# Hybrid decoder layer: the first tile's small constants, squares and turned queries put in another order

## The chip, the cores and the metric

One core of a Trainium2 chip runs the whole kernel. The metric is the device time of one execution in microseconds (us), the median of several runs; lower is better.

## What is computed

One layer of a hybrid decoder on 1024 prompt tokens and 32 sample tokens (8 sequences of 4), with a model width of 1024. What matters here is the beginning: normalise the tokens, project them to queries, keys and values, normalise each query and key head, and attend within a window of 128.

```python
def input_branches(x, norm1_g, w_in, q_norm_g, k_norm_g, ln_v_g, ln_v_b):
    h = rms_norm(x, norm1_g)
    z = jnp.einsum("bsd,de->bse", h, w_in)
    ...
    q = rms_norm(q.reshape(b, s, N_KV_HEADS, Q_GROUP, HEAD_DIM), q_norm_g)
    k = rms_norm(k.reshape(b, s, N_KV_HEADS, HEAD_DIM), k_norm_g)
...
def attn_prompt(q, k, v, sinks):
    scores = jnp.einsum("bnqkgd,bnskd->bnkgqs", qb, kk, ...) * (HEAD_DIM ** -0.5)
    p = sink_probs(scores, mask, sinks).astype(vv.dtype)
    o = jnp.einsum("bnkgqs,bnskd->bnqkgd", p, vv).reshape(b, s, ATTN_WIDTH)
```

After it come a gated spatial mixing, the merge of both branches, and a mixture of 16 experts with two per token. All of that is left as it is.

## The kernel before

The tokens are worked in nine tiles: eight of 128 prompt tokens (tile 0 to 7, `PT` is 8) and one of the 32 sample tokens. Five engines run their own instruction lists side by side and meet on semaphores; each list is written out by hand in the order in which it is issued, and an engine that waits holds up all that stands behind it in its list. SP issues the DMAs (lines 286 to 370), POOL takes the powers of -0.5 for the norms and subtracts half of the roundings, ACT copies and squares, PE multiplies and turns (transposes), DVE scales, subtracts and reduces.

Each float32 product is made of three products of reduced-precision parts (`product`, lines 65 to 74, whose three matmuls are lines 71 to 73): high by high, high by low, low by high. So each weight tile that lands is rounded by ACT into `w_hi` (line 569), and DVE makes `w_lo`, what the rounding left (lines 1034 and 1044). The weights for queries, keys and values are six tiles of 512 KB, loaded in the order `W_ORDER`: the two of keys and values, then the four of queries. Line 306 issues them. Ahead of the last two (`n == NP - 2`) SP also issues the rows of tile 1 (`load_x(1)`, line 293, which waits until ACT has normalised tile 0).

Behind the weights SP issues the transposed tokens of tile 1 (`load_xT(1)`, line 300), and then 14 small DMAs (lines 308 to 318), all on the semaphore `const_in`: the gains of the query and key norms, turned into a column one number per partition (`qk_gain`, four DMAs), the key gain and the attention sinks spread over all partitions, and the sinks of the sample tile (`s_sinks`, eight DMAs). Then come the rows and the transposed tokens of tiles 2 to 8, each behind a wait of its own: the rows of tile t reuse one buffer and wait for the squares of tile t-1 (`x_squared`).

The first tile, as the lists have it:

- PE: `first_kv` (24 matmuls), `first_q(0)` (24; the first two query weight tiles), `spread_rstd(1)`, `first_q(1)` (24; the last two), `qk_turn(0)` (four transposes of queries, one of keys; lines 722 and 723), `spread_rstd(2)`, `scores(0, 0)` (line 737). Then for each tile s from 1: `project_kv(s)`, `scores(s - 1, 1)`, `project_q(s, ...)` with the turns of the probabilities and the values of tile s-1 between its parts, `qk_turn(s)`, `dens_turn(s - 1)`, `spread_rstd(s + 2)`, `scores(s, 0)`.
- ACT: the squares of tile 0, its normalisation, the six `w_hi` with the high part of tile 0's h and the squares of tile 1 between them, `diagonal(1)` (line 493), `copy_kv(0)` (lines 517 to 522), the squares of tile 2 (`square(2)`, line 480), `h_high(1)` (line 498), `copy_q(0)` (line 506, then the squares of the queries, line 510), `diagonal(2)`, `copy_qT(0)` (line 535: the turned queries from PSUM to `qT`, times the gain), `square(3)`.
- DVE: the low parts of the weights, the last two in line 1044, then it waits for all 14 constants (line 1047), scales the query gain (line 1048), `k_squares(0)` (lines 943 and 944), `k_scale(0)`, `h_scale(1)` (line 934, eight instructions, which need tile 1's transposed tokens and its spread norm), `mean_square(2)` (line 917), `q_squares(0)`, `copy_kT(0)` (line 975). Then `mask_scores(0, 0)`, `h_scale(2)`, `mask_scores(0, 1)` and so on.
- POOL: for each s the root of the keys' squares, `rstd(s + 2)` (line 389), `h_low(s + 1)` (line 396), the root of the queries' squares (line 401).

The norm of a later tile goes a long way: ACT squares its rows, DVE takes the mean, POOL the root, ACT scales a unit matrix by it (`diagonal`), PE multiplies it by ones to spread it over the partitions (`spread_rstd`, line 660), and DVE reads that in `h_scale`.

`scores(t, gp)` works on two of the four query groups: gp 0 on groups 0 and 1, gp 1 on groups 2 and 3. It waits for `qT_copied` and for `kT_copied`. Both scores of a tile read the one `qT` that one ACT instruction fills.

Of the kernel before, what the change touches and what calls it, by code (L numbers as in the profile page):

```python
# [129 lines left out]
def attention_phase(nc, io, keep, psum):  # L130
# [7 lines left out]
    with ExitStack() as ctx:  # L138
# [148 lines left out]
        def _(sp):  # L287
# [13 lines left out]

            load_x(0)
            for n, c in enumerate(W_ORDER):
                if n == NP - 2:
                    load_x(1)
                sp.dma_start(raw[c], w_tile(io, c)).then_inc(w_in[c], DMA)
            load_xT(1)
            for half in range(2):
                part = slice(HD * half, HD * half + HD)
                sp.dma_start(qk_gain[part, 0:1], io["q_norm_g"].rearrange("a d -> d a")).then_inc(const_in, DMA)  # L310
                sp.dma_start(qk_gain[part, 1:2], io["k_norm_g"].rearrange("a d -> d a")).then_inc(const_in, DMA)
            sp.dma_start(k_gain[:, :], io["k_norm_g"][0].partition_broadcast(P)).then_inc(const_in, DMA)
            sp.dma_start(sinks[:, :], io["attn_sinks"][0].partition_broadcast(P)).then_inc(const_in, DMA)
            for g in range(G):
                for kv in range(KV):
                    h = kv * G + g
                    sp.dma_start(s_sinks[32 * g:32 * g + 32, kv:kv + 1],
                                  io["attn_sinks"][0, h:h + 1].partition_broadcast(32)).then_inc(const_in, DMA)
# [54 lines left out]
        def _(pool):  # L373
# [52 lines left out]
            for s in range(NT):  # L426
# [3 lines left out]
                if s + 2 < NT:  # L430
                    rstd(s + 2)
                if s + 1 < NT:
                    h_low(s + 1)
                if s < PT:
                    q_root(s)
                if 1 <= s <= G:
# [36 lines left out]
        def _(act):  # L473
# [50 lines left out]
            def copy_qT(t):  # L524
# [5 lines left out]

                if t < PT:
                    out = qT[:, :, 0:n]
                else:
                    out = qT[:, 0, :].rearrange("p (g n) -> p g n", g=G)
                act.activation(out, bank(psum, 4).rearrange("p (g n) -> p g n", g=G)[:, :, 0:n], ACT.Copy,
                               scale=qk_gain[:, 0:1]).then_inc(qT_copied, 1)
# [45 lines left out]
            square(2)  # L582
            for s in range(NT):
# [12 lines left out]
                else:  # L596
# [5 lines left out]
                    if s == 0:  # L602
                        copy_q(s)
                    if s + 2 < NT:
# [3 lines left out]
                    copy_qT(s)  # L608
# [32 lines left out]
        def _(pe):  # L641
# [71 lines left out]
            def qk_turn(t):  # L713
# [5 lines left out]
                if t >= 1:  # L719
                    pe.wait_ge(qT_copied, t)  # L720
# [5 lines left out]
            def scores(t, gp):  # L726
# [3 lines left out]
                pe.wait_ge(qT_copied, t + 1)  # L730
# [48 lines left out]
            def sample_scores():  # L779

                pe.wait_ge(sq_spread, 1)
                pe.wait_ge(qT_copied, NT)
# [1716 lines left out]
```

## Time and profile before

| what | us |
|---|---|
| median of three runs | 957.81 |
| lowest and highest of them | 956.85, 958.0 |
| the profiled execution's own time | 960.3 |
| its span in the trace | 958.2 |
| PE busy | 914.7 (95%) |
| DVE, ACT, POOL busy | 460.0, 356.4, 218.1 |

The span runs from the first to the last instruction of the profiled execution; 2.1 us of its own time lie around it. A busy PE is one with a matmul under way, be it at the full or the half clock. In a timeline a row is an instruction or several equal ones merged, with its start, its duration, and in brackets how long the engine was idle before it and what ended that. The mean granted clock of TensorE over the span is 0.979 of full speed.

### The profile page before, as it was taken

The page shows a single profiled execution, that of the slowest core. Times are in us where ns is not written, and L with a number is a line of the kernel's source. Part 1 is how long each engine was busy: PE and PEld are TensorE (multiplying, and loading weights), DVE is VectorE, ACT ScalarE, POOL GpSimd, SP SyncE. Part 2 cuts the span into 40 slices and gives each one's busy share as a digit, 9 for nine tenths or more (in the row PEclk, how much of TensorE's full clock was granted, in tenths as well). Part 3 has the DMA queues.
Part 4 walks back from the last instruction along what each step waited for, and adds up shares of the span by engine and source line. Part 5 has one row for each costly group of instructions (what it writes and reads, how often), then busy time and mean ns, then how long its engine had stood idle before and what let it go on. Part 6 is the DMA issues. An engine that isn't in the chain of part 4 may idle for free. (4 is left out here: it accounts for less than half of the span.)

```text
span 958.2 us, 16289 instructions
## 1 busy us (share of the span) xinstructions
PE 914.7 (95%) x5425; PEld 825.2 (86%) x5426; DVE 460.0 (48%) x842; ACT 356.4 (37%) x614; POOL 218.1 (23%) x241
## 2 busy tenths in 40 slices
PE   7899998999998999999999999999999999999993
PEld 7677776787998999999999999999887888888882
DVE  4587876433222222231232254443895768577550
ACT  5566555210232111111111141221425667577551
POOL 1434222345120000000000020000032347354552
PEclk9899999999999999999999999999899999999997
DMA  7321310200302102101110025863357898989833
GB/s 243 92 85 45 112 59 19 73 1 1 102 1 69 65 33 66 33 33 66 33 66 33 22 87 190 305 240 95 95 196 250 282 329 281 310 264 318 261 52 45
DMA packets 59247, 118.57 MB, mean 124 GB/s; under 512 B 9357, under 2 KB 34637, under 8 KB 59184
## 3 DMA queue, kind: packets, MB, share of 16 engines
q1 hardware_dynamic: 50672, 100.10, 30.4%
q0 software_dynamic: 7488, 17.85, 8.2%
q8 instruction: 28, 0.46, 0.2%
q10 hardware_dynamic: 1040, 0.00, 0.1%
q14 instruction: 19, 0.16, 0.1%
HBM read 105.37 MB, written 23.00 MB: 134 GB/s over the span
## 5 line engine op out<-in xcount | busy, mean ns | idle before, releaser
L1411 ACT ACTIVATE gate<-psum 128x352 f32<-128x352 f32 x48 | 22.2, 465 | 209.9 <-PE psum L73 209.9
L71 PE MATMUL psum<-w_hi,hT_hi 128*128 128x512 f32 (+3 forms) x224 | 84.4, 377 | 3.9 <-DVE hT_lo L1037 2.0
L73 PE MATMUL psum<-w_hi,hT_lo 128*128 128x512 f32 (+3 forms) x224 | 80.5, 359 | 0.0
L72 PE MATMUL psum<-w_lo,hT_hi 128*128 128x512 f32 (+3 forms) x224 | 80.3, 358 | 0.0
L2173 DVE TENSOR_TENSOR hT_lo<-room,hT_hi (+1 forms) x32 | 72.0, 2289 | 16.4 <-ACT hT_hi L1875 16.4
L71 PE MATMUL psum<-hT_hi,x_xT_hi 128*128 x192 | 77.5, 404 | 1.8 <-DVE x_xT_lo L2349 1.5
L71 PE MATMUL psum<-hT_hi,w_hi 128*128 128x352 f32 x240 | 77.4, 323 | 0.0
L72 PE MATMUL psum<-hT_lo,w_hi 128*128 128x352 f32 x240 | 76.9, 321 | 0.0
L73 PE MATMUL psum<-hT_hi,w_lo 128*128 128x352 f32 x240 | 76.9, 320 | 0.0
L72 PE MATMUL psum<-hT_lo,x_xT_hi 128*128 x192 | 75.2, 392 | 0.0
L73 PE MATMUL psum<-hT_hi,x_xT_lo 128*128 x192 | 75.1, 391 | 0.0
L1812 POOL DMA_INDIRECT out_y<-y,put_at x23 | 44.3, 1925 | 97.2 <-DMA out_y<-y,put_at 79.5
L1875 ACT ACTIVATE hT_hi<-room (+1 forms) x32 | 59.9, 1921 | 14.2 <-PE psum L73 12.6
L71 PE MATMUL psum<-hT_hi,g_w_hi 128*128 128x352 f32 x192 | 62.7, 326 | 2.1 <-PEq L1326 2.1
L1769 POOL MEMSET c_zeros<- 128x128 f32 x1 | 0.2, 204 | 277.7 <-POOLq L1326 277.7
L73 PE MATMUL psum<-hT_hi,g_w_lo 128*128 128x352 f32 x192 | 62.2, 324 | 0.0
L72 PE MATMUL psum<-hT_lo,g_w_hi 128*128 128x352 f32 x192 | 62.2, 324 | 0.0
L1491 DVE TENSOR_TENSOR room<-psum,gate 128x352 f32 (+1 forms) x24 | 12.5, 524 | 97.6 <-ACT gate L1411 97.6
L71 PEld LDWEIGHTS psum<-w_hi,hT_hi 128*128 128x128 f32 (+1 forms) x224 | 42.2, 188 | 15.0 <-issue 9.0
L71 PE MATMUL psum<-hT_hi,o_w_hi 128*128 128x352 f32 x168 | 54.8, 326 | 0.0
L73 PE MATMUL psum<-hT_hi,o_w_lo 128*128 128x352 f32 x168 | 54.2, 323 | 0.0
L72 PE MATMUL psum<-hT_lo,o_w_hi 128*128 128x352 f32 x168 | 54.2, 323 | 0.0
(347 smaller groups left out, 2329.6 us busy)
## 6 DMA issues: line engine op xcount, KB each, us to landing
room<-in_w_gu SPq DMA_DIRECT2D x16, 2048.0 KB
dn_raw<-in_w_dn SPq DMA_DIRECT2D x16, 1024.0 KB
g_w_raw<-in_w_ab SPq DMA_DIRECT2D x15, 768.0 KB, 4.3
xT_chunk<-in_xT SPq DMA_DIRECT2D x8, 528.0 KB, 3.7
x_in<-in_x SPq DMA_DIRECT2D x8, 512.0 KB, 4.1
out_y<-y SPq DMA_DIRECT2D x8, 512.0 KB, 3.3
hn_rows<-squares SPq DMA_DIRECT2D x8, 512.0 KB, 3.2
o_w_raw<-in_w_out_t SPq DMA_DIRECT2D x7, 512.0 KB, 6.6
```

The source lines that it names most:

```text
L71: eng.matmul(out, lh, rh, start=first and k == 0, stop=False)
L72: eng.matmul(out, lh, rl, start=False, stop=False)
L73: mm = eng.matmul(out, ll, rh, start=False, stop=last and k == nk - 1)
L1411: act.activation(gate[:, (ab + c) % 2, :], bank(psum, gate_pair(ab, c))[:, 0:TC], ACT.Sigmoid).then_inc(gated.sem, 1)
L1491: dve.tensor_tensor(out, bank(psum, gate_pair(ab, c) + 1)[:, 0:TC].unsqueeze(1), gate[:, (ab + c) % 2, :].unsqueeze(1), ALU.mult).then_inc ...
L1769: pool.memset(c["zeros"][:, :], 0.0).then_inc(zeros_made, 1)
L1812: pool.indirect_dma_start(io["y"], bass.IndirectOffsetOnAxis(put_at[:, j:j + 1], 0), out[:, j, :], None, bounds_check=NTOK - 1, oob_is_err ...
L1875: act.activation(gu_hi[:, buf, ks], gu_raw[:, buf, ks], ACT.Copy).then_inc(gu_hi_made.sem, 1)
L2173: dve.tensor_tensor(gu_lo[:, buf, ks], gu_raw[:, buf, ks], gu_hi[:, buf, ks].bitcast(F32), ALU.subtract).then_inc(gu_lo_made.sem, 1)
```

## The change

- SP: the 14 small DMAs move from behind `load_xT(1)` to between `load_x(1)` and the last two query weight tiles.
- ACT: `square(2)` moves from ahead of `h_high(1)` to behind `copy_q(0)` and `copy_qT(0)`; in the first tile `copy_qT(0)` also comes ahead of `diagonal(2)`.
- ACT: `copy_qT` of a prompt tile is two instructions, two groups each; `scores(t, gp)` waits for its own half (`u + 1` is 2t + gp + 1). The other waits on `qT_copied` are renumbered.
- DVE: `mean_square(2)` moves from ahead of `q_squares(0)` to behind `copy_kT(0)`. POOL: `rstd(2)` moves behind `h_low(1)` and the root of tile 0's queries. PE: `spread_rstd(2)` moves from ahead of `scores(0, 0)` to behind `project_kv(1)`.
- The condition `0 < s < NT - 2` on POOL's first `rstd` leaves all tiles but s = 0 as they were.

```diff
--- before.py
+++ after.py
@@ -299,23 +299,26 @@
                     sp.wait_ge(h_scaled, 2 * (t - 1))
                 sp.dma_start(xT_tile[t % 2][:, :, 0:rows(t)], io["xT"][:, :, toks(t)]).then_inc(xT_came[t % 2], DMA)
 
+            def load_constants():
+                for half in range(2):
+                    part = slice(HD * half, HD * half + HD)
+                    sp.dma_start(qk_gain[part, 0:1], io["q_norm_g"].rearrange("a d -> d a")).then_inc(const_in, DMA)
+                    sp.dma_start(qk_gain[part, 1:2], io["k_norm_g"].rearrange("a d -> d a")).then_inc(const_in, DMA)
+                sp.dma_start(k_gain[:, :], io["k_norm_g"][0].partition_broadcast(P)).then_inc(const_in, DMA)
+                sp.dma_start(sinks[:, :], io["attn_sinks"][0].partition_broadcast(P)).then_inc(const_in, DMA)
+                for g in range(G):
+                    for kv in range(KV):
+                        h = kv * G + g
+                        sp.dma_start(s_sinks[32 * g:32 * g + 32, kv:kv + 1],
+                                      io["attn_sinks"][0, h:h + 1].partition_broadcast(32)).then_inc(const_in, DMA)
+
             load_x(0)
             for n, c in enumerate(W_ORDER):
                 if n == NP - 2:
                     load_x(1)
+                    load_constants()
                 sp.dma_start(raw[c], w_tile(io, c)).then_inc(w_in[c], DMA)
             load_xT(1)
-            for half in range(2):
-                part = slice(HD * half, HD * half + HD)
-                sp.dma_start(qk_gain[part, 0:1], io["q_norm_g"].rearrange("a d -> d a")).then_inc(const_in, DMA)
-                sp.dma_start(qk_gain[part, 1:2], io["k_norm_g"].rearrange("a d -> d a")).then_inc(const_in, DMA)
-            sp.dma_start(k_gain[:, :], io["k_norm_g"][0].partition_broadcast(P)).then_inc(const_in, DMA)
-            sp.dma_start(sinks[:, :], io["attn_sinks"][0].partition_broadcast(P)).then_inc(const_in, DMA)
-            for g in range(G):
-                for kv in range(KV):
-                    h = kv * G + g
-                    sp.dma_start(s_sinks[32 * g:32 * g + 32, kv:kv + 1],
-                                  io["attn_sinks"][0, h:h + 1].partition_broadcast(32)).then_inc(const_in, DMA)
             for t in range(2, NT):
                 load_x(t)
                 load_xT(t)
@@ -427,12 +430,14 @@
                 if s == PT:
                     q_root(s)
                 k_root(s)
-                if s + 2 < NT:
+                if 0 < s < NT - 2:
                     rstd(s + 2)
                 if s + 1 < NT:
                     h_low(s + 1)
                 if s < PT:
                     q_root(s)
+                if s == 0:
+                    rstd(s + 2)
                 if 1 <= s <= G:
 
                     pool.wait_ge(z_rstd, 2 * s + 2)
@@ -528,12 +533,14 @@
                 if t >= 1:
                     act.wait_ge(s_made, 2 * t)
 
+                src = bank(psum, 4).rearrange("p (g n) -> p g n", g=G)
                 if t < PT:
-                    out = qT[:, :, 0:n]
+                    for gp in range(2):
+                        gs = slice(2 * gp, 2 * gp + 2)
+                        act.activation(qT[:, gs, :], src[:, gs, :], ACT.Copy, scale=qk_gain[:, 0:1]).then_inc(qT_copied, 1)
                 else:
-                    out = qT[:, 0, :].rearrange("p (g n) -> p g n", g=G)
-                act.activation(out, bank(psum, 4).rearrange("p (g n) -> p g n", g=G)[:, :, 0:n], ACT.Copy,
-                               scale=qk_gain[:, 0:1]).then_inc(qT_copied, 1)
+                    act.activation(qT[:, 0, :].rearrange("p (g n) -> p g n", g=G), src[:, :, 0:n], ACT.Copy,
+                                   scale=qk_gain[:, 0:1]).then_inc(qT_copied, 1)
 
             def probs(t, gp):
                 u = 2 * t + gp
@@ -579,7 +586,6 @@
                 act.activation(w_hi[:, :, c * P:(c + 1) * P], vs_raw[c], ACT.Copy).then_inc(vs_hi_made, 1)
 
             copy_kv(0)
-            square(2)
             for s in range(NT):
                 done = s - 1
                 if s == PT:
@@ -601,11 +607,13 @@
                     h_high(s + 1)
                     if s == 0:
                         copy_q(s)
+                        copy_qT(s)
+                        square(s + 2)
                     if s + 2 < NT:
                         diagonal(s + 2)
                     if s > 0:
                         copy_q(s)
-                    copy_qT(s)
+                        copy_qT(s)
                     if s > 0:
                         copy_rT(done)
                     if s + 3 < NT:
@@ -717,7 +725,7 @@
                 if t == PT:
                     pe.wait_ge(sq_normed, 1)
                 if t >= 1:
-                    pe.wait_ge(qT_copied, t)
+                    pe.wait_ge(qT_copied, 2 * t)
                 for g in range(G):
                     pe.transpose(bank(psum, 4)[:, g * P:g * P + n], z[0:n, g * P:(g + 1) * P], ident[0:n, 0:n])
                 pe.transpose(bank(psum, 1)[:, KT_AT:KT_AT + n], k_norm[0:n, :, :].rearrange("p k d -> p (k d)"),
@@ -727,7 +735,7 @@
 
                 u = 2 * t + gp
                 k0 = block_keys(t)
-                pe.wait_ge(qT_copied, t + 1)
+                pe.wait_ge(qT_copied, u + 1)
                 pe.wait_ge(kT_copied, t + 1)
                 if u >= 1:
                     pe.wait_ge(s_ready, u)
@@ -779,7 +787,7 @@
             def sample_scores():
 
                 pe.wait_ge(sq_spread, 1)
-                pe.wait_ge(qT_copied, NT)
+                pe.wait_ge(qT_copied, 2 * PT + 1)
                 pe.wait_ge(kT_copied, NT)
                 pe.wait_ge(k_cache_in, DMA)
                 pe.wait_ge(s_ready, 2 * PT)
@@ -855,10 +863,11 @@
             spread_rstd(1)
             first_q(1)
             qk_turn(0)
-            spread_rstd(2)
             scores(0, 0)
             for s in range(1, PT):
                 project_kv(s)
+                if s == 1:
+                    spread_rstd(s + 1)
                 scores(s - 1, 1)
                 project_q(s, 0, 4)
                 probs_turn(s - 1, 0)
@@ -1055,7 +1064,7 @@
             def spread_q():
 
                 dve.wait_ge(spread_zeroed, 1)
-                dve.wait_ge(qT_copied, NT)
+                dve.wait_ge(qT_copied, 2 * PT + 1)
                 dve.tensor_scalar(spread(qT_spread), bank(psum, 4).rearrange("p (g n) -> p g n", g=G)[:, :, 0:NS]
                                   .rearrange("p g (b t) -> p b g t", b=DEC_B), qk_gain[:, 0:1], None,
                                   ALU.mult).then_inc(sq_spread, 1)
@@ -1063,9 +1072,9 @@
             k_squares(0)
             k_scale(0)
             h_scale(1)
-            mean_square(2)
             q_squares(0)
             copy_kT(0)
+            mean_square(2)
             for s in range(1, NT):
                 done = s - 1
                 mask_scores(done, 0)
```

## Rows read from the trace of the kernel before

**Rows 1.** The page: busy time of each engine, and the chain that ended last.

```profile
PE 914.7 (95%) x5425; PEld 825.2 (86%) x5426; DVE 460.0 (48%) x842; ACT 356.4 (37%) x614; POOL 218.1 (23%) x241
...
PE 36%; DVE 2%; DMA 1%; issue 1%; POOL 0%; ACT 0%; DVEq 0%; POOLq 0%; ACTq 0%
```

**Rows 2.** Timeline of PE: start us, us, instruction [idle before <-releaser].

```profile
19.63 0.36 PE L71 MATMUL psum<-w_hi,hT_hi 128*128 128x256 f32 x1
...
22.48 0.27 PE L73 MATMUL psum<-w_hi,hT_lo 128*128 128x256 f32 x1
26.30 0.79 PE L722 MATMUL psum<-ident,z_qkv 128*128 128x128 f32 x4 [3.54 <-ACT z_qkv L506]
...
28.68 1.23 PE L737 MATMUL psum<-kT,qT 64*128 64x128 f32 x8 [0.63 <-DVE kT L975]
...
34.50 0.72 PE L737 MATMUL psum<-kT,qT 64*128 64x128 f32 x8
...
45.18 1.14 PE L737 MATMUL psum<-kT,qT 64*128 64x256 f32 x8 [0.46 <-ACT qT L535]
```

**Rows 3.** Timeline of ACT in the first tile.

```profile
16.31 1.06 ACT L569 ACTIVATE w_hi<-sp_sb 128x1024 fp32r<-128x1024 f32 x1 [0.33 <-DMA sp_sb<-in_w_tiles]
...
23.20 1.06 ACT L480 ACTIVATE x_in<-x_in 128x1024 f32<-128x1024 f32 x1 [4.51 <-DMA x_in<-in_x]
...
25.13 0.63 ACT L498 ACTIVATE hT_hi<-h_raw 128x512 fp32r<-128x512 f32 x1 [0.26 <-DVE h_raw L934]
25.67 0.58 ACT L506 ACTIVATE z_qkv<-psum 128x512 f32<-128x512 f32 x1
...
27.34 0.69 ACT L535 ACTIVATE qT<-psum,qk_gain 128x512 f32<-128x512 f32 x1
...
34.61 0.28 ACT L517 ACTIVATE z_qkv<-psum 128x128 f32<-128x128 f32 x1 [5.53 <-PE psum L73]
```

**Rows 4.** Timeline of DVE in the first tile.

```profile
16.11 2.52 DVE L1044 TENSOR_TENSOR w_lo<-sp_sb,w_hi 128x1024 fp32r<-128x1024 f32 x2
21.38 0.15 DVE L1048 TENSOR_SCALAR qk_gain<-qk_gain 128x1 f32<-128x1 f32 x1 [2.75 <-DMA s_sinks<-in_attn_sinks]
...
22.95 2.15 DVE L934 SCALAR_TENSOR_TENSOR h_raw<-x_in,g,psum 128x128 f32<-128x128 f32 x8
...
28.19 0.34 DVE L975 TENSOR_SCALAR kT<-psum,qk_gain 128x128 f32<-128x128 f32 x1
```

**Rows 5.** Timeline of SP's queue: one row is the issue of one or several DMAs.

```profile
7.73 0.33 SPq L293 DMA_DIRECT2D x_in<-in_x  x1
8.10 0.91 SPq L306 DMA_DIRECT2D sp_sb<-in_w_tiles  x2
...
9.76 2.27 SPq L310 DMA_DIRECT2D qk_gain<-in_q_norm_g  x1
...
15.13 3.68 SPq L317 DMA_DIRECT2D s_sinks<-in_attn_sinks  x8
18.86 0.42 SPq L293 DMA_DIRECT2D x_in<-in_x  x1
```

**Rows 6.** DMA issues: rows of tile 3 at 24.38, xT of tile 2 at 19.32; us to landing.

```profile
x_in<-in_x SPq DMA_DIRECT2D x1, 512.0 KB, 3.5
...
x_norm<-in_xT SPq DMA_DIRECT2D x1, 512.0 KB, 5.5
```

**Rows 7.** Stretches of PE: length, busy (instructions), granted clock, DMA share, GB/s.

```profile
13.00:16.40 3.40, 3.40 (x19) 0.50 0.90 270
26.60:33.40 6.80, 6.17 (x31) 0.51 0.57 189
```

**Rows 8.** Timelines of ACT, DVE and PE around the turn of tile 2.

```profile
60.88 0.69 ACT L535 ACTIVATE qT<-psum,qk_gain 128x512 f32<-128x512 f32 x1 [0.45 <-PE psum L723]
...
61.27 0.34 DVE L975 TENSOR_SCALAR kT<-psum,qk_gain 128x128 f32<-128x128 f32 x1
...
61.71 1.14 PE L737 MATMUL psum<-kT,qT 64*128 64x256 f32 x8 [0.20 <-ACT qT L535]
```

## The prediction

> **What bounds the kernel now.** I began with the page's busy times and its chain [rows 1]: PE is busy for 95% of the span, and of the chain only PE has a share that counts. So any microsecond by which PE's list is moved in the first tile is passed on to the end, as long as no wait further on takes it up. Next I read PE's timeline of the first tile [rows 2]. PE has its third product (`first_q(1)`) done at 22.75 us, then stands idle until 26.30, where the turn starts on ACT's copy of the queries. From there to `scores(0, 0)` at 28.68 it is idle again for 0.63 us, on DVE's copy of the turned keys.
>
> Why is that copy late? ACT's timeline [rows 3] has it at 25.67, right behind the second half of h of tile 1. Ahead of that ACT waited 4.51 us for tile 2's rows (23.20), whose squares stand in its list. But h of tile 1 came only when DVE had scaled it: DVE's timeline [rows 4] has the last low part of the weights done at 18.63, then 2.75 us of waiting for the constants, the gain at 21.38 and the eight scalings from 22.95 to 25.10. Both waits have one root: SP's queue [rows 5]. The constants are issued from 9.76 to 18.81, 9.05 us for 14 DMAs, the first alone 2.27. Tile 2's rows, free to go since tile 1's squares, go behind them at 18.86. So SP's time of issue is what the first tile pays for. The constants land late for DVE, the rows late for ACT, and DVE's chain is the one that ends last.
>
> **The moved constants.** The 14 issues now stand ahead of the last two weight tiles, which SP issued at 8.10 (both in 0.91 us). For the 14, my bounds are 9.05 us as measured and 7.24 us, which has the first at the 0.46 us of a sink's issue (3.68 / 8 in [rows 5]; 9.05 - 2.27 + 0.46). I take the short one: the 2.27 came when six loads had been issued ahead of it and few were through, now there are fewer. The last weight tile is then issued at 8.10 + 7.24 + 0.45 = 15.8 us, at the latest at 17.6, where it was 8.55. It lands 3.5 us later if it goes as fast as a load alone, 5.5 if like the second of a pair [rows 6]. It is the second of a pair, with tile 1's transposed tokens behind it, so I take 5.5. Call the landing L: 21.3 us, between 19.3 and 23.1. Before, ACT had it at 16.31.
>
> The Trainium skill, "DMA: Bandwidth & Descriptors", section "Issuing engines are not separate DMA queues", says that the time to initiate a DMA on its sequencer is usually small beside the DMA itself. By that the move would delay the weights hardly at all. The rows above say otherwise here for small transfers, but it is the second rival below.
>
> What hangs on L: DVE has the last low part 2.32 us after ACT starts on the tile (16.31 to 18.63), so `first_q(1)`, which began at 19.63 without a wait for weights, now begins at L + 2.4 = 23.7, after 4 us of idle PE. It took 3.0 us at the full clock. The granted clock was 0.50 from 13.0 to 16.4 after an idle stretch of 2 us, and again from 26.6 to 33.4 after the 3.54 us [rows 7]. So this product will run mostly at the half clock, 1.2 GHz. `project_kv(1)`, as many matmuls, took 4.6 us mostly at that level (29.91 to 34.50 in [rows 2]). I take 4.6, which gives queries at L + 7.0. Ends: 3.0 and, all doubled, 6.0.
>
> The other chain: the constants are in by then, so DVE takes up the gain at L + 2.3. From the gain to the end of `h_scale(1)` is 25.10 - 21.38 = 3.7 us [rows 4], then 0.57 for ACT's last half of h [rows 3]: ACT could copy the queries at L + 6.6. `copy_kv(0)` now also stands behind the late weight tile on ACT, and is done before DVE is free, so it adds nothing. Tile 1's transposed tokens are issued at 16.3 and needed at L + 3.9 = 25.2, which is 9 us. The later of both chains is PE's: the copy starts at L + 7.1 = 28.4 against 25.67, **+2.7 us**. With the bounds of L and 6.6 to 8.5 behind it, the copy lies between +0.2 and +5.9.
>
> **The squares, the diagonal and the rest of tile 2's norm.** The squares leave ACT's way ahead of h: that was a wait of 4.51 us, but its cover was DVE's late h, so it is worth 0 (the second half waited for DVE by 0.26 as it was). With the copy of the keys unchanged in its place, from ACT's copy of the queries to `scores(0, 0)` stays 28.68 - 25.67 = 3.0 us. `diagonal(2)` ahead of `copy_qT(0)` cost nothing, since that copy began at 27.34 as the turn ended. `spread_rstd(2)` leaves PE ahead of the scores, where PE waited for keys anyway: 0. What is late next: `square(3)` waits in ACT's list for rows that are issued only after `square(2)`, now about when the scores begin, and land 3.5 us later [rows 6]. `copy_kv(1)` stands behind it. In the trace it came 5.9 us after the scores (34.61 in [rows 3]), which leaves room for the 3.5 and the 1.06 of the squares. Only when PE is fast does this bite, by 0 to 0.4 us. `h_scale(2)` on DVE now waits for a matmul behind `project_kv(1)`; what DVE does next, `mask_scores(0, 1)`, needs scores that PE makes behind that same product and so waited there before too: 0.
>
> **The halved copy of the queries.** It can bring only what `scores` waits for `qT` beyond `kT`. At tile 2 `qT` is done at 61.57 and `kT` at 61.61 [rows 8], PE goes at 61.71: the wait of 0.20 that the trace puts down to ACT ends with DVE. The tiles repeat this, with waits of 0.2 (0.46 at tile 1, [rows 2]), and by their order `kT` hangs on the squares of the queries, which the change doesn't touch. So **0**; if the attribution were right, at most the 0.3 us by which half a copy of 0.69 is shorter, at seven tiles: 2.1 us at the very most, 1.6 by the waits that there are (0.46 and six times 0.2). The second instruction lengthens ACT's list by 0.1 to 0.2 us a tile, which ACT's idle time covers (37% busy in [rows 1]).
>
> **What the clock gives back.** After `scores(0, 0)` PE ran on at the half clock until 33.4: those scores took 1.23 where the second ones took 0.72, `project_kv(1)` 4.6 where `first_q(1)` took 3.0. Together that is 2.1 us. If PE's new burst from 23.7 to 28.3 brings the full clock back in time, all of it comes back, less the 0.4 of `square(3)`; if the idle stretches around the turn take it away once more, nothing does. I take 1.2, between the ends 0 and 2.1.
>
> **Sum.** +2.7 - 1.2 + 0 = +1.5 us on 960.3 for the profiled execution, which stood 2.5 above the median. On the median it is 957.81 + 1.5 = **959.3**. A measurement of this kernel tells 0.2% from nothing, 1.9 us, so the forecast case is "the same, rather slower".
>
> **Rivals.**
> 1. *The queue stalls as before* (slower). The first constant takes its 2.27 us again, behind x of tile 1 and two weight tiles in flight, L is 23.1, and PE's longer idle leaves the half clock on through `project_kv(1)`. Then +2.7 + 1.8 - 0 to 1.2: +3.3 to +4.5, or 961.1 to 962.3. For it: the 9.05 us is what was measured. It decides from 0.4 us above my sum. Chance 0.27.
> 2. *The weights don't wait* (faster). If issuing were cheap here, as by the skill's rule, the last tile would land as at 16.3, `first_q(1)` would end at 22.75, and the early constants would give DVE's chain 2.75 us. ACT copies at 22.9, -2.8, and with no idle PE the clock stays, up to -2.1 more: 952.9 to 955.0. Against it: SP issued tile 2's rows only behind the last constant, though nothing else held them. Chance 0.10.
> 3. *Early landing and a quick clock*: L at 19.3 to 20 and all 2.1 us back, -1.9 to +0.1, or 955.9 to 957.9. Chance 0.15.
> The forecast case, 0 to +3.2, has 0.48.
>
> **The numbers.** Slower by over 0.2%: 0.27 and the upper quarter of the forecast case, 0.12, is 0.39. Faster by over 0.2%: 0.10 and 0.04 of the third rival, 0.14. Between: 0.47. The range leaves out the second rival and the last part of the first: 956.4 to 962.3. The forecast case alone is 957.8 to 961.0.
>
> **What would show it.** In the changed trace: SP issues the last two weight tiles at 15 to 17.6 us; ACT's `w_hi` of the last starts at L; PE idle of about 4 us ahead of the second half of the queries' product, with a granted clock near 0.50 after it; DVE's wait for constants gone, its wait for the last weights in its place; `copy_q(0)` at 28.4, the scores at 31.4. The step is wrong if SP's issues take well under 7 us, or if the last tile lands before 19. The clock term is right if the start of `scores(1, 0)`, 45.18 before [rows 2], moves by about 1.5. From there on all tiles should keep their 16.5 us (61.71 - 45.18), with waits before `scores` of the same 0.2; if those waits vanish, the halved copy did count.

## The result, and the profile after

The changed kernel takes 961.2 us in the median of 20 runs (958.32 to 963.19), the kernel before 958.8 in 20 runs beside them (956.85 to 961.33). The ratio is 1.0021, 95% interval 1.0012 to 1.003: 2.0 us slower, with 1.2 to 2.9 as its bounds (the two medians lie 2.4 us apart). A second comparison gave 1.0012 (0.9995 to 1.0029), which by itself is not clear of nothing.

The profiled execution doesn't show this by itself. It took 960.29 us (span 958.1), as long as the one of before (960.3, span 958.2); before's was 1.5 us above its own median, after's 0.9 below. So first what its parts show, then which of them lasts. The page:

```profile
PE 912.1 (95%) x5425; PEld 822.3 (86%) x5426; DVE 460.9 (48%) x842; ACT 357.2 (37%) x622; POOL 225.2 (24%) x241
...
PE 36%; DVE 2%; DMA 1%; issue 1%; POOL 0%; ACT 0%; DVEq 0%; POOLq 0%; ACTq 0%
```

PE is the bound as in [rows 1]. SP's queue, which answers to [rows 5]:

```profile
7.77 0.33 SPq L293 DMA_DIRECT2D x_in<-in_x  x1
...
8.14 0.58 SPq L305 DMA_DIRECT2D qk_gain<-in_q_norm_g  x1
...
11.77 3.70 SPq L312 DMA_DIRECT2D s_sinks<-in_attn_sinks  x8
...
15.51 0.90 SPq L320 DMA_DIRECT2D sp_sb<-in_w_tiles  x2
...
17.10 0.66 SPq L293 DMA_DIRECT2D x_in<-in_x  x1
```

The 14 constants take from 8.14 to 15.47, 7.3 us, the first of them 0.58 and not 2.27. The last two weight tiles go at 15.51 where they went at 8.10. ACT and DVE, which answer to [rows 3, 4]:

```profile
19.19 1.06 ACT L576 ACTIVATE w_hi<-sp_sb 128x1024 fp32r<-128x1024 f32 x1 [5.30 <-DMA sp_sb<-in_w_tiles]
...
20.54 1.06 ACT L576 ACTIVATE w_hi<-sp_sb 128x1024 fp32r<-128x1024 f32 x1 [0.30 <-DMA sp_sb<-in_w_tiles]
...
27.27 0.60 ACT L511 ACTIVATE z_qkv<-psum 128x512 f32<-128x512 f32 x1
...
28.73 0.84 ACT L540 ACTIVATE qT<-psum,qk_gain 128x256 f32<-128x256 f32 x2 [0.20 <-PE psum L731]
...
33.98 1.06 ACT L485 ACTIVATE x_in<-x_in 128x1024 f32<-128x1024 f32 x1 [1.83 <-DMA x_in<-in_x]
```

```profile
20.27 2.58 DVE L1053 TENSOR_TENSOR w_lo<-sp_sb,w_hi 128x1024 fp32r<-128x1024 f32 x2 [4.04 <-ACT w_hi L576]
...
22.77 0.15 DVE L1057 TENSOR_SCALAR qk_gain<-qk_gain 128x1 f32<-128x1 f32 x1
...
24.33 2.15 DVE L943 SCALAR_TENSOR_TENSOR h_raw<-x_in,g,psum 128x128 f32<-128x128 f32 x8
...
29.37 0.34 DVE L984 TENSOR_SCALAR kT<-psum,qk_gain 128x128 f32<-128x128 f32 x1
```

ACT's wait has changed its name. It was 4.51 us for tile 2's rows at 23.20; it is 5.30 us for a weight tile at 19.19. DVE's wait of 2.75 us for the constants is gone, and a wait of 4.04 for the weights stands ahead of 20.27. The gain comes at 22.77, 1.4 us later than before. PE, which answers to [rows 2], and its granted clock, which answers to [rows 7]:

```profile
21.94 0.62 PE L668 MATMUL psum<-qT_spread 128*128 128x128 f32 x2 [2.55 <-ACT qT_spread L498]
...
23.00 0.55 PE L71 MATMUL psum<-w_hi,hT_hi 128*128 128x256 f32 x1 [0.44 <-DVE w_lo L1053]
...
27.93 0.66 PE L730 MATMUL psum<-ident,z_qkv 128*128 128x128 f32 x4 [0.69 <-ACT z_qkv L511]
...
29.86 0.72 PE L745 MATMUL psum<-kT,qT 64*128 64x128 f32 x8 [1.17 <-DVE kT L984]
...
33.77 0.71 PE L745 MATMUL psum<-kT,qT 64*128 64x128 f32 x8
...
44.53 1.14 PE L745 MATMUL psum<-kT,qT 64*128 64x256 f32 x8 [0.46 <-ACT qT L540]
```

```profile
22.20:25.60 3.40, 2.96 (x14) 0.50 0.84 260
26.60:33.40 6.80, 4.95 (x43) 1.00 0.24 77
```

PE's idle stretch now lies ahead of the second half of the queries' product, and the half clock (1.2 GHz) falls on that product, from 22.2 to 25.6. `project_kv(1)`, which ran at the half clock before [rows 7], runs at the full one (2.4 GHz). So `scores(0, 0)` starts 1.18 us later than before, and `scores(1, 0)` 0.65 earlier (44.53 against 45.18).

### The profile page after: what moved, and what is told of

The parts are those of the page before. It is cut to its first block and busy times, and to the rows that moved or that the text cites. A ratio compares the mean times of both kernels' runs of the same rounds, so it can differ in the third digit from the quotient of the medians.

```text
span 958.1 us, 16297 instructions
## 1 busy us (share of the span) xinstructions
PE 912.1 (95%) x5425; PEld 822.3 (86%) x5426; DVE 460.9 (48%) x842; ACT 357.2 (37%) x622; POOL 225.2 (24%) x241
## 5 line engine op out<-in xcount | busy, mean ns | idle before, releaser
L1420 ACT ACTIVATE gate<-psum 128x352 f32<-128x352 f32 x48 | 22.2, 464 | 210.1 <-PE psum L73 210.0
L1821 POOL DMA_INDIRECT out_y<-y,put_at x23 | 46.5, 2023 | 89.7 <-DMA out_y<-y,put_at 71.0
```

Source lines behind the costliest of these rows:

```text
L1420: act.activation(gate[:, (ab + c) % 2, :], bank(psum, gate_pair(ab, c))[:, 0:TC], ACT.Sigmoid).then_inc(gated.sem, 1)
L1821: pool.indirect_dma_start(io["y"], bass.IndirectOffsetOnAxis(put_at[:, j:j + 1], 0), out[:, j, :], None, bounds_check=NTOK - 1, oob_is_err ...
```

## The experiments

All traces in one table, in us. "S0" is the start of `scores(0, 0)`, "S1" that of `scores(1, 0)`; between them lie 16.50 us in [rows 2]. The ratios are to the kernel before, run on the same chip.

| kernel | gain on DVE | S0 | S1 | S1 - S0 | median (runs) | ratio (95%) |
|---|---|---|---|---|---|---|
| before, first trace | 21.38 | 28.68 | 45.18 | 16.50 | 958.8 (20) | |
| before again | 20.41 | 28.70 | 45.72 | 17.02 | 960.38 (12) | 1.0013 (0.999 to 1.0036) |
| after, first trace | 22.77 | 29.86 | 44.53 | 14.67 | 961.2 (20) | 1.0021 (1.0012 to 1.003) |
| after again | 22.73 | 30.02 | 45.77 | 15.75 | 959.96 (11) | 1.0012 (0.9995 to 1.0029) |
| constants alone | 22.72 | 30.03 | 44.40 | 14.37 | 961.12 (7) | 1.0035 (1.002 to 1.005) |
| all but the constants | 19.98 | 26.83 | 42.96 | 16.13 | 958.86 (12) | 1.0007 (0.9996 to 1.0019) |
| half copies alone | 19.59 | 27.09 | 43.70 | 16.61 | 959.56 (12) | 1.0014 (1.0003 to 1.0024) |
| after, six constants ahead | 19.60 | 26.45 | 43.66 | 17.21 | 958.39 (12) | 0.9993 (0.9977 to 1.0009) |
| before, PE kept busy | 20.26 | 27.57 | 41.93 | 14.36 | 954.49 (6) | 0.9958 (0.9942 to 0.9973) |
| after, PE kept busy | 22.61 | 29.79 | 44.37 | 14.58 | 958.45 (11) | 0.9995 (0.9987 to 1.0004) |
| constants on ACT | 20.33 | 29.07 | 45.97 | 16.90 | 961.65 (11) | 1.002 (1.0005 to 1.0035) |
| the same, PE kept busy | 20.51 | 29.26 | 43.63 | 14.37 | 960.52 (12) | 1.0012 (1.0001 to 1.0022) |
| sinks late | 19.24 | 27.89 | 43.71 | 15.82 | 958.34 (11) | 0.9991 (0.9978 to 1.0004) |
| the same, PE kept busy | 18.40 | 27.07 | 41.44 | 14.37 | 955.61 (8) | 0.9961 (0.9947 to 0.9975) |

The kernel before against itself reads 1.0013, with an interval that holds 1. Differences of 0.1% between two lines are therefore not to be read. The traces' times of S0 and S1 are finer, but each is one execution, and S0 of one and the same kernel differs by the landing of its loads.

### The change taken apart

Constants alone: the 14 DMAs are moved as in the change, nothing else is.

```diff
                 if n == NP - 2:
                     load_x(1)
+                    load_constants()
...
-            for half in range(2):
...
```

> Only the 14 constants are moved ahead of the last two weight tiles. Theory A (the weights are late because SP's issues take 7.4 us): all of the change's loss is here, +1.2 to +3 us against before (ratio 1.001 to 1.003), the last weight tile starts on ACT at 20 to 21 us, scores(0, 0) at about 29.9 where it was 28.68. Rival B (the loss comes from tile 2's later norm or from the two half copies): no slower than before, ratio 0.998 to 1.0005.

All of the loss is here: 1.0035, a little above the forecast range, with S0 at 30.03 and the last weight tile on ACT at 20.49. That is theory A's case, and B falls. S1, at 44.40, is as early as in the changed kernel and earlier than before's 45.18, so the loss that the medians show is not to be seen at S1 of this trace.

All but the constants: `load_constants()` is called behind `load_xT(1)`, as the 14 were before (the edit is against the changed kernel).

```diff
                     load_x(1)
-                    load_constants()
...
             load_xT(1)
+            load_constants()
```

> All of the change except for the constants, which stay behind the transposed tokens of tile 1. Theory A: within 0.5 us of before, since DVE still waits for the constants until 21.4 us and ACT's copy of the queries hangs on that (25.6 to 25.7 us). Rival B: +1 to +2.5 us, with copies or norms late at each tile. A third reading (ACT's wait of 4.5 us for tile 2's rows was what held the copy): -1 us or more, the copy well before 25 us.

No loss (1.0007). But S0 is at 26.83, 1.85 us earlier than in before, and the copy of the queries at 24.27, where theory A had 25.6. The first trace of before was a late one, it turned out: here the last constant was there at 19.98, not 21.38, and from the gain to the copy it is 4.29 us in both. So this trace doesn't tell whether ACT's wait for the rows (the third reading) counts. The kernel before, unchanged, for a second trace:

> The kernel before, unchanged, against itself, for a second profile: ratio 1 within 0.001. The first trace has the last constant at 21.4 us; the parts' traces, with the same SP order, have it at 19.6 to 20.3. If that first trace was a late one: the gain at 19.5 to 20.5 here, scores(0, 0) at 26.8 to 27.6. If the first was typical: 21.4 and 28.7.

The gain came early, at 20.41, and S0 did not follow: 28.70, as in the first trace. The rows of this trace (timelines of DVE, ACT and PE):

```profile
20.41 0.15 DVE L1048 TENSOR_SCALAR qk_gain<-qk_gain 128x1 f32<-128x1 f32 x1 [1.92 <-DMA s_sinks<-in_attn_sinks]
...
23.84 1.06 ACT L480 ACTIVATE x_in<-x_in 128x1024 f32<-128x1024 f32 x1 [3.98 <-DMA x_in<-in_x]
...
25.94 0.57 ACT L506 ACTIVATE z_qkv<-psum 128x512 f32<-128x512 f32 x1
...
26.56 0.66 PE L722 MATMUL psum<-ident,z_qkv 128*128 128x128 f32 x4 [3.83 <-ACT z_qkv L506]
...
28.70 1.22 PE L737 MATMUL psum<-kT,qT 64*128 64x128 f32 x8 [0.69 <-DVE kT L975]
```

DVE is through with h of tile 1 at 24.13, but ACT waited 3.98 us for tile 2's rows and squared them until 24.9. Then came two halves of h and only then the queries, at 25.94. With the squares out of the way ACT could have copied them 0.57 us behind DVE's h, at 24.7: the squares held the copy by 1.2 us. So in the kernel before two waits are nearly level, the constants' and the squares', and which ends last differs from one execution to the next. Where the squares are moved (all but the constants) S0 was at 26.83; where they are not and the rows came early (half copies alone, ACT's squares at 21.94) at 27.09, as DVE's chain allows.

Half copies alone: only `copy_qT` and its waits.

```diff
+                    for gp in range(2):
+                        gs = slice(2 * gp, 2 * gp + 2)
+                        act.activation(qT[:, gs, :], src[:, gs, :], ACT.Copy, scale=qk_gain[:, 0:1]).then_inc(qT_copied, 1)
...
-                pe.wait_ge(qT_copied, t + 1)
+                pe.wait_ge(qT_copied, u + 1)
```

> Only the turned queries of a prompt tile are copied in two halves. By the prediction 0 (within 0.3 us): scores hang on the turned keys, and the waits before scores stay 0.2 and 0.46 us. If the trace's attribution of these waits to the queries were right: up to -1.6 us, and the waits gone. If ACT's longer list counts: up to +1 us.

```profile
42.61 0.84 ACT L535 ACTIVATE qT<-psum,qk_gain 128x256 f32<-128x256 f32 x2 [0.19 <-PE psum L725]
...
43.26 0.34 DVE L977 TENSOR_SCALAR kT<-psum,qk_gain 128x128 f32<-128x128 f32 x1
...
43.70 1.13 PE L739 MATMUL psum<-kT,qT 64*128 64x256 f32 x8 [0.47 <-ACT qT L535]
```

Two instructions take 0.84 us where one took 0.69, and the wait of 0.47 before the scores of tile 1 is what it was (0.46 in [rows 2]): it ends with DVE's turned keys (43.26 + 0.34). From the scores of tile 1 to those of tile 7 it is 99.20 us in the traces of before and after and 99.22 here, so a tile neither gains nor loses. The ratio, 1.0014, leans to the slow side; nothing in this trace answers to that, and the kernel before reads the same against itself.

The changed kernel, unchanged, for a second trace:

> The changed kernel, unchanged, for a second profile on a chip with the kernel before: scores(0, 0) at 29.7 to 30.1 again, since its end hangs on SP's issues and not on the last constant; ratio 1.001 to 1.003. Rival: it spreads as the first trace of before did, and the ratio is 1 within 0.001.

S0 is at 30.02, beside 29.86: the changed kernel's first tile hardly spreads, as its end hangs on SP's issues. What spreads is the stretch behind it, 15.75 us in place of 14.67:

```profile
31.91 0.41 ACT L498 ACTIVATE qT_spread<-ident,xrs 128x128 f32<-128x128 f32 x1 [1.15 <-POOL xrs L392]
...
35.20 1.06 ACT L485 ACTIVATE x_in<-x_in 128x1024 f32<-128x1024 f32 x1 [2.89 <-DMA x_in<-in_x]
...
36.26 0.26 ACT L522 ACTIVATE z_qkv<-psum 128x128 f32<-128x128 f32 x1
...
38.57 0.66 PE L756 MATMUL psum<-ident,sp_sb 128*128 128x128 f32 x4 [0.93 <-ACT sink_e L554]
```

ACT waits 2.89 us for tile 3's rows, which are issued only when tile 2's are squared. The copy of tile 1's keys stands behind them at 36.26, the probabilities behind that, and PE waits 0.93 us ahead of their turn. In the first trace of after the same wait was 1.83 us and PE had none there. This is the moved squares' own price; with the constants alone, where the squares were not moved, S1 - S0 is 14.37.

### How much of the weights' delay is SP's time of issue

The changed kernel with only six constants ahead of the weights; the eight sinks, which the sample tile alone needs, follow `load_xT(2)` on a semaphore of their own.

```diff
-        N_CONST = 6 + G * KV
+        N_CONST = 6
...
+            def load_sinks():
                 for g in range(G):
...
                 load_xT(t)
+                if t == 2:
+                    load_sinks()
...
+            dve.wait_ge(sinks_in, DMA * G * KV)
             step.did(dve.tensor_tensor(top[:, 0:KV], s_top[:, :], s_sinks[:, :], ALU.max))
```

> The changed kernel, but only the 6 constants that the first tile needs are ahead of the last two weight tiles; the 8 sinks of the sample tile go behind the transposed tokens of tile 2, on a semaphore of their own. Theory A: the issues ahead of the weights fall from 7.4 to 3.5 us, the last weight tile is there at 16.5 to 17.5 us (the DMA engines are then the limit), DVE starts on the gain at about 19.5, scores(0, 0) at 26 to 27 us: 2 to 4 us faster than before (ratio 0.996 to 0.998). Rival B: no faster than before.

```profile
11.75 0.91 SPq L323 DMA_DIRECT2D sp_sb<-in_w_tiles  x2
...
17.36 1.06 ACT L581 ACTIVATE w_hi<-sp_sb 128x1024 fp32r<-128x1024 f32 x1 [0.29 <-DMA sp_sb<-in_w_tiles]
...
19.60 0.15 DVE L1062 TENSOR_SCALAR qk_gain<-qk_gain 128x1 f32<-128x1 f32 x1
...
24.51 0.66 PE L735 MATMUL psum<-ident,z_qkv 128*128 128x128 f32 x4 [1.59 <-ACT z_qkv L516]
...
26.45 1.23 PE L750 MATMUL psum<-kT,qT 64*128 64x128 f32 x8 [1.17 <-DVE kT L989]
```

```profile
25.60:32.40 6.80, 5.96 (x30) 0.50 0.49 152
```

SP's part came out as theory A had it: 3.8 us less of issue, the last tile 3.2 us earlier (17.36 against 20.54), S0 3.4 us earlier. The time did not come out as expected: 0.7 us faster than before and not clear of it, where 2 to 4 were expected. Against the changed kernel's 1.0021 it is 2.7 us better, so the eight sinks ahead of the weights carry the loss. PE's idle stretches (1.59 ahead of the turn, 1.17 ahead of the scores) now lie behind the queries' product again, and the half clock falls on the scores and on `project_kv(1)`, 25.6 to 32.4. S1 is at 43.66, so S1 - S0 took 17.21 us, 2.85 more than in the traces at the full clock below (14.36). Of the 3.4 us that the weights' earlier landing gained at S0 over the changed kernel, 0.9 are left at S1 (43.66 against 44.53).

### The clock held still

To see the late weights without the half clock behind them, PE is kept busy in its idle stretches by matmuls of the unit matrix by itself into an unused bank (`warm_up`, which the kernel has for its start). Nothing reads their result. In the kernel before:

```diff
             first_q(1)
+            warm_up(14)
             qk_turn(0)
             spread_rstd(2)
+            warm_up(4)
             scores(0, 0)
```

> The kernel before, with 14 matmuls of the unit matrix by itself in PE's idle stretch ahead of the turn of tile 0 and 4 ahead of its first scores (their result is not used). They are to keep the full clock. Theory A: from scores(0, 0) to scores(1, 0) takes 14.4 us in place of 16.5, as in the changed kernel, and the kernel is 1 to 2 us faster than before (ratio 0.998 to 0.999). If the half clock costs nothing at the end: within 0.5 us of before.

```profile
25.65 0.60 PE L722 MATMUL psum<-ident,z_qkv 128*128 128x128 f32 x4
...
27.57 0.72 PE L737 MATMUL psum<-kT,qT 64*128 64x128 f32 x8
...
31.25 0.72 PE L737 MATMUL psum<-kT,qT 64*128 64x128 f32 x8
...
41.93 1.13 PE L737 MATMUL psum<-kT,qT 64*128 64x256 f32 x8 [0.47 <-ACT qT L535]
```

```profile
26.60:33.40 6.80, 6.75 (x56) 1.00 0.47 145
```

The clock stays at 1.00 where it was 0.51 in [rows 7], S1 - S0 is 14.36 in place of 16.50, and the kernel takes 954.49 us: ratio 0.9958, 4 us faster, twice the most that was expected. S0, at 27.57, is early for another reason than the clock: the constants and tile 2's rows were there early (the gain at 20.26, the squares at 22.01), and from the copy of the queries to S0 it is 3.0 us as in the first trace of before. This trace also lacks a stretch of half clock near 170 us that the first traces of before and after both have (0.50 from 170.0 and from 168.9, for 3.4 us each); behind it 1.6 us more are gained. Whether that comes of the new order in time or of chance, one trace doesn't tell. The profiled execution (953.06 us) was also the fastest of its six.

In the changed kernel, where the idle stretches are others:

```diff
+            warm_up(18)
             spread_rstd(1)
             first_q(1)
+            warm_up(4)
             qk_turn(0)
+            warm_up(7)
             scores(0, 0)
```

> The changed kernel, with 18 such matmuls ahead of spread_rstd(1), 4 ahead of the turn and 7 ahead of scores(0, 0). With the clock kept up in both, what is left between this and the kernel before with its own such matmuls is the late weights alone. Theory A: 2.5 to 3 us slower than that one, with scores(0, 0) at 29.5 to 30 us, and about level with before (ratio 0.9995 to 1.0015). Rival (the change's loss was the clock's): level with the kernel before that has them.

```profile
27.53 0.66 PE L730 MATMUL psum<-ident,z_qkv 128*128 128x128 f32 x4
...
29.79 0.71 PE L745 MATMUL psum<-kT,qT 64*128 64x128 f32 x8
...
44.37 1.13 PE L745 MATMUL psum<-kT,qT 64*128 64x256 f32 x8 [0.46 <-ACT qT L540]
```

S0 is where it was (29.79), S1 too. Side by side on one chip, both at the full clock between S0 and S1, the two orders differ by 2.2 us at S0, 2.4 at S1 and 4.0 in the medians (954.49, 958.45), where 2.5 to 3 were expected. What the medians have beyond the 2.4 lies behind S1: the trace of the changed kernel has the stretch of half clock near 170 us, and the other hasn't. The rival, that the change's loss was the clock's, falls: with PE kept busy in both the changed order is still the slower one, and by more.

### Other places for the constants

Six constants issued by ACT at its very start, where it waits for tile 0's rows, and the sinks late as above, without and with PE kept busy (4 ahead of the turn, 4 ahead of the scores).

```diff
             act.dma_start(g1[:, :], io["norm1_g"][0].rearrange("(k p) -> p k", p=P)).then_inc(g1_in, DMA)
+            for half in range(2):
+                part = slice(HD * half, HD * half + HD)
+                act.dma_start(qk_gain[part, 0:1], io["q_norm_g"].rearrange("a d -> d a")).then_inc(const_in, DMA)
...
```

> The kernel before, with the 6 constants of the first tile issued by ACT at its start, where it waits for tile 0's rows, and the 8 sinks of the sample tile behind the transposed tokens of tile 2 on SP. Nothing stands ahead of the weights, and DVE waits for no constant. Theory A: the last weight tile on ACT at 15 to 16.5 us, the gain at 18.7, the copy of the queries at 22.9, scores(0, 0) at 25.5: 1.5 to 3 us faster than before (ratio 0.997 to 0.9985). It fails if ACT's six issues (3.5 us) hold up the squares of tile 0, which begin at 4.5: then later by that much.

> The same as the one with ACT's constants, with 4 matmuls of the unit matrix ahead of the turn and 4 ahead of scores(0, 0). Theory A: clock kept up, scores(1, 0) at about 40 us where the kernel before has 43 to 45: 3 to 5 us faster than before (ratio 0.995 to 0.997). If the clock stays up without them: the same as without.

```profile
5.17 1.28 ACT L485 ACT_TABLE_LOAD   x1 [5.02 <-issue]
...
6.47 1.06 ACT L485 ACTIVATE x_norm<-x_in 128x1024 f32<-128x1024 f32 x1
```

ACT's issues last until 5.14, and the load of its table, which used to run while the rows were on their way, comes only then: the squares of tile 0 start at 6.47 and not at 4.52. Tile 0 starts 1.95 us late. The expectation had named this as what could spoil it. Without the added matmuls the kernel is slower than before (1.002). With them it is not faster (1.0012, no more than before reads against itself), and the first tile does not explain that: S1 is at 43.63, 1.55 us earlier than in the first trace of before, and that lead is still 1.58 us among the last experts (an ACT copy at 887.39 that stood at 888.97). It goes just behind:

```profile
895.05 1.03 ACT L1935 ACTIVATE y<-psum 128x1024 f32<-128x1024 f32 x1 [3.56 <-POOLq L1819]
```

In the first trace of before this row stands at 893.68, behind a wait of 0.61. ACT copies an expert's output here, and may do so only when POOL has seen its last scatter-add into `y` land. Behind it, at PE's last wait for an expert (943.08 against 941.14), the lead of 1.6 us has become a lag of 1.9. A lead of the first tile can so be spent at the end, on a DMA; that this wait alone did it was not tried.

Six constants left on SP behind the weights, as before, and only the sinks late, without and with PE kept busy:

> The same order of the constants without the added matmuls. Theory A: scores(0, 0) at 25.5 to 26 as there; PE's idle stretches are shorter than before (about 1 us and 1 us), so the half clock may or may not come: 1.5 to 4 us faster than before (ratio 0.996 to 0.9985).

> The kernel before, with the 8 sinks of the sample tile behind the transposed tokens of tile 2 and the 6 other constants left behind the weights, and with 4 matmuls of the unit matrix ahead of the turn and 4 ahead of scores(0, 0). The sixth constant is issued by 14 us and lands before 18.5, so DVE takes up the gain at 18.5 to 18.7, ACT copies the queries at 22.7 to 23.0, scores(0, 0) begins at 25.5 to 26 and scores(1, 0) at about 40: 5 to 6 us faster than before (ratio 0.9935 to 0.9955). If the constants' place is of no account and only the clock is: like the kernel before with its 18 such matmuls, ratio 0.9958.

With PE kept busy the gain comes at 18.40, the rows of tile 2 at 19.67, and yet S0 is 27.07 and not 25.5 to 26 (27.89 without, where all is 0.8 us later from tile 0's h on). The rows of the one kept busy (timelines of POOL, ACT and DVE), and then POOL's row in the changed kernel:

```profile
16.05 2.35 DVE L1051 TENSOR_TENSOR w_lo<-sp_sb,w_hi 128x1024 fp32r<-128x1024 f32 x2
...
16.22 2.60 POOL L394 TENSOR_TENSOR xrs<-xss,minus_half 128x1 f32<-128x1 f32 x1 [9.75 <-DVE xss L924]
...
18.85 0.40 ACT L498 ACTIVATE qT_spread<-ident,xrs 128x128 f32<-128x128 f32 x1 [2.57 <-POOL xrs L394]
...
18.40 0.15 DVE L1055 TENSOR_SCALAR qk_gain<-qk_gain 128x1 f32<-128x1 f32 x1
...
21.33 2.15 DVE L941 SCALAR_TENSOR_TENSOR h_raw<-x_in,g,psum 128x128 f32<-128x128 f32 x8
```

```profile
16.32 0.55 POOL L392 TENSOR_TENSOR xrs<-xss,minus_half 128x1 f32<-128x1 f32 x1 [9.75 <-DVE xss L926]
```

The root of tile 1's norm takes POOL 2.60 us while DVE subtracts weights beside it (16.05 to 18.40), and 0.55 where DVE stands idle. ACT's list waits 2.57 us for it, and the squares of tile 0's keys behind it are done by 19.8, so `h_scale(1)` starts at 21.33, three microseconds behind the gain. This third wait is what bounds the first tile once the constants and the squares are out of the way. It is close behind them in the kernel before as well: with half copies alone the gain was at 19.59 and `h_scale(1)` at 21.36, so constants that come earlier than that bring nothing. The kernel with PE kept busy reads 0.9961, where 0.9935 to 0.9955 was expected, level with the kernel before kept busy (0.9958); without the added matmuls it is 0.9991, not clear of nothing. The constants' place brought 0.5 us at S0 and nothing that the runs tell.

The Trainium skill, "SBUF — State Buffer", "Who interferes with whom", says that a DVE instruction with two inputs from SBUF contends with a GpSimd instruction that reads SBUF, and that the order of issue decides which of the two is blocked. The rows agree with that in kind: 2.60 us beside DVE's subtractions of two operands from SBUF, 0.55 without them. In the first trace of before it was 1.46 beside the same subtractions, which then took 2.52 us in place of 2.35.

## Why the prediction was right, and where it was not

**The total.** 959.3 was forecast, 1.5 us above the median then known, within 956.4 to 962.3; measured were a ratio of 1.0021 (2.0 us) and a median of 961.2. The sign and the size hold, and 2.0 us lies in the forecast case (0 to +3.2). The median itself lies 0.2 us above that case's upper end of 961.0, since the 20 runs of the kernel before have a median of 958.8 and not 957.81. That the sum came out so near is in part luck. It was a sum for S1, said to move by +1.5 us, and S1 moved by -0.65 between the first traces and by +0.05 between the second ones; its steps were off with opposite signs.

**The moved constants.** Right as a mechanism and nearly in size. The issues took 7.3 us (7.24 forecast; the first at 0.58), the last two tiles went at 15.5. L was 20.54, not 21.3: the second of the pair landed in 4.6 us, between the bounds of 3.5 and 5.5. The product of the queries began at 23.00 (L + 2.5), was to take 4.6 and took 4.1, and the copy came at 27.27, not 28.4. There the two chains were level, as DVE's chain alone had it at L + 6.6 = 27.1. The copy's delay was +1.6 us in the first traces, forecast +2.7. The step from the copy to S0, taken as 3.0, was 2.6: DVE's `TENSOR_SCALAR` on the squares of the queries, ahead of the turned keys, takes 0.17 us where it took 0.61. In before POOL is at the low parts of h(1) beside it (until 28.25), as the root of tile 2's norm stands ahead of them; in after they are done at 28.71. Against the copy's delay, the trace of before had its last constant late, at 21.38 where four others had it at 19.6 to 20.4. The four traces that have before's order of constants and squares have S0 at 27.09 to 28.70, 28.0 in the mean; the four with all constants ahead have it at 29.79 to 30.03, 29.9 in the mean. So the late weights cost 1.9 us at S0, between 1.1 and 2.9; that is the number to keep.

**The squares worth 0.** This reading of the kernel before failed. I had read them as hidden by DVE's late h, by 0.26 us of a wait in one trace. A cover that thin held in one execution and not in the next: in the second trace of before DVE's h was there at 24.1, and ACT's squares held the copy until 25.94. Moving them is a gain of up to 1.2 us there. In the changed kernel, whose weights are late, the 0 holds: with the constants alone, squares unmoved, S0 is at 30.03, beside 29.86 and 30.02. What was said to be late next, `square(3)`, was right in its place and undersized: 0 to 0.4 us forecast, 0.2 to 1.4 measured (S1 - S0 of 14.58, 14.67 and 15.75 against 14.36), with a wait of PE of 0.93.

**The halved copy.** Right: 0, tile by tile, and the waits of 0.2 and 0.46 stay, since they end with the turned keys.

**The clock.** Right in kind, undersized in the traces; what the prediction asked for as its sign, S1 moved by about 1.5 us, did not come (-0.65 and +0.05). The half clock fell on the queries' product, where DVE's chain hides most of it, and left `project_kv(1)`: 1.8 us came back in the first traces, forecast 1.2; between the second ones 1.3, `square(3)` included. Its whole price behind S0 is 2.1 to 2.9 us (16.50 to 17.21 against 14.36). With PE kept busy in both kernels, the change costs 2.4 us at S1 instead of nothing; some of that is the one trace of before, whose rows and constants were early (S0 at 27.57, where the mean of four is 28.0).

**The rivals.** The queue that stalls as before did not show: in the kernel before the first constant took 2.27 us to issue (2.54 in its second trace), behind two weight tiles and the transposed rows of tile 1; ahead of the tiles it took 0.58. Weights that don't wait are refuted by 5.30 us of ACT's wait. The Trainium skill's sentence beside that rival ("DMA: Bandwidth & Descriptors", "Issuing engines are not separate DMA queues"), that the time to initiate a DMA is usually small beside the DMA itself, agrees for a weight tile (0.45 us of issue, 4.6 to landing) and less for these 14 (0.43 to 0.60 us of issue each, 1.8 to 3.3 from issue to landing). It is their sum in one queue, 7.3 us, that the last weight tiles wait for.

**Open.** At S1 the three traces with the constants ahead (44.40, 44.53, 45.77) and the three with the kernel before's order of constants and squares (43.70, 45.18, 45.72) average the same, 44.9 us. The 2.0 us of the medians must then come, at least in part, from executions other than those profiled, or from behind S1. The traces show two things there. One is ACT's wait for POOL's scatter among the last experts: in the first trace of after it is 1.39 us (0.61 in before), the lead over before is 1.08 us ahead of it (887.89 against 888.97) and 0.49 behind it (940.65 against 941.14), and the two spans end within 0.1 us of each other. No run was made to move that wait. The other is the clock. Stretches of half clock come and go: near 300 us one was there in both second traces and with six constants ahead, in none of the first ones; near 170 us it lasted 6.8 us in the second trace of after and 3.4 in the first ones. Whether the shift of the first tile moves them in a fixed way was not tried and isn't shown.

## What to carry to other kernels

Small DMAs are paid for in their issuing queue: 14 constants of 0.1 to 32 KB held SP for over 7 us, so count the issues ahead of what is urgent, and move to the back those that only a later stage needs. Before an idle stretch of PE is shortened or moved, look at which product then meets the half clock; filling the stretch with matmuls was worth 2.5 to 4 us in three of the four orders tried (0.8 in the one with the constants on ACT), more than any place of the constants brought against the kernel before (0.9 us at most, and not clear of nothing). And a wait that another one covers by a few tenths of a microsecond in one trace is not hidden: take a second trace before you put it at nothing.

## What had not been expected

- Keeping PE busy with 18 matmuls of the unit matrix made the kernel before 0.42% faster (0.9958, where 0.998 to 0.999 was expected), faster than both kernels of this study.
- The same source, run again, had the constants 1.0 us earlier (20.41 against 21.38) and the rows of tile 2 0.6 us later (23.84 against 23.20), though the first of the constants took longer to issue in that second trace (2.54 us against 2.27): the time from issue to landing isn't a fixed one. The first tile's end in the kernel before is set by whichever comes last.
- POOL's root of one column took 2.60 us beside DVE's subtractions and 0.55 without them (and 1.46 in the first trace of before).
- Issues of DMAs put ahead of ACT's first activation hold up its table load: 1.95 us of tile 0's start for six constants.
